# Attention operands split once and kept in DRAM, attention results in a buffer of their own, in a decoder-trunk kernel on one core

## What is computed

```python
def cross_attention(h, mem_n, wq, wk, wv, wo):
    ...
    s = jnp.einsum("bthd,bmhd->bhtm", q, k).astype(jnp.float32) * (XATTN_HEAD_DIM ** -0.5)
    p = jax.nn.softmax(s, axis=-1).astype(h.dtype)
    o = jnp.einsum("bhtm,bmhd->bthd", p, v).reshape(b, t, XATTN_HEADS * XATTN_HEAD_DIM)
    return o @ wo

def reference(...):
    ...
    h = rms_norm(x, xattn_pre_norm[l])
    y = cross_attention(h, mem_n, xattn_wq[l], xattn_wk[l], xattn_wv[l], xattn_wo[l])
    x = x + rms_norm(y, xattn_post_norm[l])
```

## Time and profile before

| | |
|---|---|
| time, 3 runs | 2698.38 us median (2696.05 to 2699.09) |
| profiled execution, its time | 2691.14 us |
| its span, first to last instruction | 2689.3 us |
| PE busy | 2549.9 us (95%) |
| DVE busy | 1579.4 us (59%) |
| ACT busy | 966.0 us (36%) |
| POOL busy | 982.5 us (37%) |
| mean granted TensorE clock | 0.984 of full speed |
| the four attention tiles | 782.72 to 1197.19 us of the span |

### The profile page before, as it was taken

The page is one execution under the profiler, slowest core; times in us unless marked ns, Lnnn a source line. Parts: engine busy times, 40 slices in busy tenths (PEclk is TensorE's granted clock), DMA queues, the critical chain, the costliest instruction groups (busy, mean ns, idle before and its releaser), DMA issues.

```text
span 2689.3 us, 33390 instructions
## 1 busy us (share of the span) xinstructions
PE 2549.9 (95%) x11713; PEld 2114.1 (79%) x11713; DVE 1579.4 (59%) x2446; ACT 966.0 (36%) x1565; POOL 982.5 (37%) x394
## 2 busy tenths in 40 slices
PE   7869899999998998999999999999999999999997
PEld 6657788878877787777888878888878888778886
DVE  4898888777736547447626456346276264562462
ACT  5323322232235444453433433333434334233332
POOL 6451400000023443333444444534444444345342
PEclk9989999999999999999999999999999999999999
DMA  8785585665834524435333244332353332443331
GB/s 243 232 317 196 196 302 177 240 251 209 307 125 172 195 79 179 166 95 185 95 110 94 81 142 147 109 94 95 87 189 96 107 94 84 133 128 107 91 94 63
DMA packets 318417, 410.59 MB, mean 153 GB/s; under 512 B 12584, under 2 KB 235069, under 8 KB 305469
## 3 DMA queue, kind: packets, MB, share of 16 engines
q1 hardware_dynamic: 309709, 396.62, 44.3%
q10 hardware_dynamic: 8560, 12.06, 1.3%
HBM read 343.62 MB, written 65.01 MB: 152 GB/s over the span
## 4 chain that ended last, share of the span: by engine, by line
PE 77%; DVE 14%; issue 5%; ACT 2%; DMA 1%; POOL 1%; DVEq 0%; ACTq 0%; SPq 0%; POOLq 0%
PE colb L1411 15%; PE colb L1413 15%; PE colb L1412 15%; PE accb L1411 10%; PE accb L1413 10%; PE accb L1412 10%; DVE arena L1147 3%; PE colb L1448 2%; DVE xh L1087 1%; DVE arena L1310 1%; DVE xh L1014 1%; DVE small L1008 1%; DVE small L1301 1%; ACT junk L656 1%; POOL pair L604 1%
## 5 line engine op out<-in xcount | busy, mean ns | idle before, releaser
L604 POOL TENSOR_TENSOR pair<-raw,pair 128x1024 fp32r<-128x1024 f32 x387 | 981.6, 2551 | 1676.2 <-ACT pair L635 1676.0
L1411 PE MATMUL colb<-hT,pair 128*128 128x512 f32 x1952 | 765.8, 392 | 18.8 <-issue 15.5
L1413 PE MATMUL colb<-hT,pair 128*128 128x512 f32 x1952 | 762.2, 390 | 0.0
L1412 PE MATMUL colb<-hT,pair 128*128 128x512 f32 x1952 | 762.0, 390 | 0.0
L635 ACT ACTIVATE pair<-raw 128x1024 fp32r<-128x1024 f32 x387 | 406.0, 1054 | 541.9 <-PE accb L1413 314.5
L1354 DVE TENSOR_SCALAR arena<-arena,par 128x512 f32<-128x512 f32 x176 | 246.1, 1438 | 375.5 <-ACT arena L938 375.0
L1411 PE MATMUL accb<-pair,act 128*128 128x512 f32 x1120 | 440.2, 393 | 18.7 <-issue 6.2
L1411 PEld LDWEIGHTS colb<-hT,pair 128*128 128x128 f32 x1952 | 368.3, 189 | 102.8 <-issue 27.1
L1413 PE MATMUL accb<-pair,act 128*128 128x512 f32 x1120 | 437.3, 390 | 0.0
L1412 PE MATMUL accb<-pair,act 128*128 128x512 f32 x1120 | 436.9, 390 | 0.0
L1413 PEld LDWEIGHTS colb<-hT,pair 128*128 128x128 f32 x1952 | 367.9, 188 | 77.5
(11 more groups left out here) (150 smaller groups left out, 2395.2 us busy)
## 6 DMA issues: line engine op xcount, KB each, us to landing
raw<-in_ffn_w_up SPq DMA_DIRECT2D x176, 512.0 KB, 3.8
pair<-kept SPq DMA_DIRECT2D x75, 1024.0 KB, 4.9
raw<-in_ffn_w_down SPq DMA_DIRECT2D x176, 256.0 KB, 2.9
kept<-pair SPq DMA_DIRECT2D x25, 1024.0 KB, 5.1
raw<-att_a SPq DMA_DIRECT2D x64, 256.0 KB, 3.0
raw<-att_b SPq DMA_DIRECT2D x64, 256.0 KB, 5.9
raw<-in_w_in SPq DMA_DIRECT2D x17, 512.0 KB, 6.6
xh<-in_x SPq DMA_DIRECT2D x4, 2048.0 KB, 14.2
```

Source lines behind the costliest of these rows:

```text
L604: nc.gpsimd.tensor_tensor(pair[:, b, 1, :], raw[:, r, :], pair[:, b, 0, :].bitcast(F32), ALU.subtract).then_inc(lo_done, 1)
L1411: nc.tensor.matmul(dst, sh, mh, start=first, stop=False)
L1412: nc.tensor.matmul(dst, sh, ml, start=False, stop=False)
L1413: return nc.tensor.matmul(dst, sl, mh, start=False, stop=last)
```

## The change

The 16 attention slots become kept slots too. The first attention tile is a stage of its own (`ATT_FIRST`): it loads and splits the slots as before, and SP stores each finished pair to `kept` (1 MB). The other three (`ATTN`) have no `hi` and no `lo`: SP loads the finished pair, as soon as PE has used the slot that had the buffer. Results go to `y_att`, a new part of the arena, and `xh` is loaded by `next_attended` in the tile before. In all tiles the first probability transposes come after slot 6 in place of slot 5. In `ATTN` the next rows' squares and scaling come before the exponentials and the first low parts, and their transposes one slot earlier; in `ATT_FIRST` their squares come after the rounding of the second transposes.

```diff
+    ORDER = {..., **{p: [("s", i) for i in range(2 * KD)] for p in ATTS}}
+    TILES = [1, 1, NT - 2, 1, 1, NT - 1, NT]
+    KEPT = [...] + [("s", i) for i in range(2 * KD)]
+    kept_in = {what: {"c": PREP, "s": ATT_FIRST}.get(what[0], MIX_FIRST) for what in KEPT}
+    HEADS_AT = {ATT_FIRST: 2, ATTN: 1}
+        y_att = part([RB, D])
...
+            def next_attended(tile):
+                sp.wait_ge(x_new, step_tile.at(ATT_FIRST, 0, 1))
+                sp.wait_ge(xp_full, xp.at(ATTN, tile - 1, 0) if tile else xp.at(ATT_FIRST, 0, 0))
+                if tile < NT - 1:
+                    sp.wait_ge(x_stored, 16 * (tile + 3))
+                    src = rows(x_mixed, tile + 1)
+                else:
+                    sp.wait_ge(x_stored, 16 * (2 + NT))
+                    src = rows(x_attended, 0)
+                sp.dma_start(xh[:, :, :], src).then_inc(xh_in, 16)
...
-                    if p == MIX_FIRST and i + LOAD_AHEAD - RAWS + 1 < SLOTS[p]:
+                    kept_next = i + LOAD_AHEAD - RAWS + 1
+                    if p in (MIX_FIRST, ATT_FIRST) and kept_next < SLOTS[p] or p == MIX_LAST and kept_next >= SLOTS[p]:
                         keep(p, t, i + LOAD_AHEAD - RAWS + 1)
                     load(p, t, i + LOAD_AHEAD, last)
+                    if p in ATTS and i == 9 and tile_of(p, t) < NT - 1:
+                        next_attended(tile_of(p, t) + 1)
...
-            for p in (MIX, MIX_LAST, ATTN, FFN):
+            for p in (MIX, MIX_LAST, ATT_FIRST, FFN):
                 with pool.Fori(0, TILES[p]) as t:
                     for n in range(len(SPLIT[p])):
                         lo(p, t, n)
...
                 for i in range(2 * KD):
-                    hi(ATTN, t, i + AHEAD)
+                    hi(p, t, i + AHEAD)
+                    if i == 2 and p == ATTN:
+                        next_squares(p, t)
                     if i == 3:
                         exps(0)
-                    if i == 5:
+                    if i == 6:
                         for k in range(4):
...
-                    if i == 6:
-                        next_squares(ATTN, t)
...
+                    if i == 8 and p == ATT_FIRST:
+                        next_squares(p, t)
...
-                take_rows(ATTN, t, 9, 15, 1, PV1_USE, xh)
+                take_rows(p, t, 9, 15, 1, PV1_USE, y_att)
...
                 normalise(0)
+                if p == ATTN:
+                    next_rows(p, t)
                 for k in range(4):
...
-                    if i == 5:
-                        pe.wait_ge(prob_ready, probs.at(ATTN, t, RB))
+                    if i == 6:
+                        pe.wait_ge(prob_ready, probs.at(p, t, RB))
```

More of the change, by code:

```diff
@@ L35 @@
 RSQRT_SEED = float(0x5F3759DF)
-PREP, MIX_FIRST, MIX, MIX_LAST, ATTN, FFN = range(6)
+PREP, MIX_FIRST, MIX, MIX_LAST, ATT_FIRST, ATTN, FFN = range(7)
 MIXES = (MIX_FIRST, MIX, MIX_LAST)
+ATTS = (ATT_FIRST, ATTN)
 RAWS = 4
@@ L131, in build @@
     KEPT = [("c", i) for i in range(CSLOTS)] + [("r", i) for i in range(RSLOTS)] +\
-           [("out", half, j) for half in range(2) for j in range(KD // 2)]
-    kept_in = {what: PREP if what[0] == "c" else MIX_FIRST for what in KEPT}
+           [("out", half, j) for half in range(2) for j in range(KD // 2)] + [("s", i) for i in range(2 * KD)]
+    kept_in = {what: {"c": PREP, "s": ATT_FIRST}.get(what[0], MIX_FIRST) for what in KEPT}
     def ready_made(p, i):
@@ L156, in stores_of @@
     def stores_of(b, p, i):
-        return 16 * sum(keeps(q, j) and pair_of[q][j] == b for q in (PREP, MIX_FIRST) for j in range(SLOTS[q]) if (q, j) < (p, i))
+        return 16 * sum(keeps(q, j) and pair_of[q][j] == b for q in (PREP, MIX_FIRST, ATT_FIRST) for j in range(SLOTS[q]) if (q, j) < (p, i))
     pool0, conf0, gate0 = 0, NP_, NP_ + NC_
@@ L199, in slot_source @@
                 return cols(w_in[0], REST_CHUNKS[n])
+            if what == "s":
+                half, j = divmod(n % KD, KD // 2)
+                return rows(lambda k: (att_a, att_b)[n // KD], (0, 2 * j, half), (0, 2 * j + 1, half))
             if what == "pooled":
@@ L208, in slot_source @@
             return rows(lambda k: pooled_w_out if k < NP_ else w_out[0], (0, Y_ORDER[2 * j], n), (0, Y_ORDER[2 * j + 1], n))
-        if p == ATTN:
-            half, j = divmod(i % KD, KD // 2)
-            return rows(lambda k: (att_a, att_b)[i // KD], (0, 2 * j, half), (0, 2 * j + 1, half))
         q, j = divmod(i, SLOTS[FFN] // 2)
@@ L223, in earlier @@
         if p > PREP and i < size:
-            before = bufs[p - 1] + bufs[p][:i]
+            before = sum(bufs[:p], []) + bufs[p][:i]
             d = min(d, next((e for e in range(1, 2 * size + 1) if before[-e] == own[j]), d))
@@ L412, in build @@
         pool_step = sem("pool_step")
-        nmaxs = Plan([0, 0, 0, 0, 8, 0], TILES)
-        probs = Plan([0, 0, 0, 0, 8, 0], TILES)
-        sigs = Plan([0, NC_, NC_, NC_, 0, 0], TILES)
-        sums = Plan([1, 1, 1, 0, 0, 0], TILES)
-        pairs = Plan([0] * 5 + [KF], TILES)
-        heads = Plan([2] + [1] * 5, TILES)
-        squares = Plan([M // P + RB] + [RB + 8] * 5, TILES)
+        nmaxs = Plan([0, 0, 0, 0, 8, 8, 0], TILES)
+        probs = Plan([0, 0, 0, 0, 8, 8, 0], TILES)
+        sigs = Plan([0, NC_, NC_, NC_, 0, 0, 0], TILES)
+        sums = Plan([1, 1, 1, 0, 0, 0, 0], TILES)
+        pairs = Plan([0] * 6 + [KF], TILES)
+        heads = Plan([2] + [1] * 6, TILES)
+        squares = Plan([M // P + RB] + [RB + 8] * 6, TILES)
         def result_squares(p, t):
@@ L541, in store_rows @@
                 sp.dma_start(rows(target[p], tile), xt[:, :, :]).then_inc(x_stored, 16)
+            def next_attended(tile):
[8 more added lines that the diff above has]
+                sp.dma_start(xh[:, :, :], src).then_inc(xh_in, 16)
             def body(p, t):
-                last = isinstance(t, int)
+                last = isinstance(t, int) and t == TILES[p] - 1
                 for i in range(SLOTS[p]):
@@ L557, in body @@
                         sp.dma_start(gain[:, :], post_gain[p][0].partition_broadcast(P)).then_inc(gain_in, 16)
-                        if not (last and p == FFN):
+                        if p not in ATTS and not (last and p == FFN):
                             sp.wait_ge(xp_full, xp.at(p, t, 0))
@@ L585, in _ @@
             body(MIX_LAST, 0)
-            for p in (ATTN, FFN):
-                with sp.Fori(0, NT - 1) as t:
-                    body(p, t)
-                body(p, NT - 1)
+            body(ATT_FIRST, 0)
+            for t in range(NT - 1):
+                body(ATTN, t)
+            with sp.Fori(0, NT - 1) as t:
+                body(FFN, t)
+            body(FFN, NT - 1)
             sp.wait_ge(x_stored, 16 * (1 + 3 * NT - 1 + RB))
@@ L1320, in attn @@
                 for k in range(4, KD):
[L1321 to L1322 removed]
+                    lo_acc(p, t, k, k % RB, act[:, 1, k, :], act[:, 0, k, :])
+                if p == ATT_FIRST:
+                    next_rows(p, t)
                 for k in range(KD):
[L1324 to L1325 removed]
+                    lo_acc(p, t, KD + k, k % RB, hT[:, 1, k, :], hT[:, 0, k, :], par_at[next_pre(p, t)] + k)
+                new_rows(p, t, y_att)
                 end()
[L1328 to L1330 removed]
+            attn(ATT_FIRST, 0)
+            with ve.Fori(0, NT - 2) as t:
+                attn(ATTN, t)
+            attn(ATTN, NT - 2)
             nc.vector.memset(halo[:, :, :], 0.0).then_inc(conv_ready, 1)
```

139 lines of the change are left out of this document (69 added, 70 removed).

## The result

| | before | changed |
|---|---|---|
| time, 4 runs each | 2697.22 us median (2694.32 to 2699.09) | 2663.03 us median (2660.64 to 2665.46) |
| profiled execution, its time | 2691.14 us | 2663.32 us |
| span | 2689.3 us | 2661.0 us |
| ratio changed/before | | 0.9874, 95% interval 0.9861 to 0.9888 |

The changed kernel is 34 us (1.3%) faster, by the interval 30 to 37 us. Repeated beside 23 and 9 fresh runs of the kernel before, the ratio was 0.9886 and 0.9889, which is 31 and 30 us. (One later execution of the changed kernel, of 5100.91 us, stands apart from all others, and the ratios leave it out.)

The account below looks back on a forecast made before the run. PE, 95% busy, was taken to bound the kernel, delayed by DVE, which POOL's splits slow. Tiles 1 to 3 give 26.0 us, tile 0 1.6: 2698.4 - 27.6 = 2670.8 us, range 2664 to 2684.

Parts of the forecast that it names:

- The lower end of the range: Whole kernel, 2664 us: all tiles at 94.6 would be 36 us less, tile 0's chain cuts that to 34.
- the 0.2 us: Tiles 1 to 3, PE's wait for `normalise(1)` before the second transposes: 0.2 us a tile counted, 0.5 kept as bound.
- The new wait for `xh`: Tile 0, PE before the next rows' transposes, their squares now coming later: 4.1 us, 6.5 or 2 as bounds.
- The second wait: Tile 0, PE before the second probability transposes: 2.2 us before, 1.2 us taken to stay, bounds 0 and 2.5.
- the first wait: PE before the first probability transposes, for `normalise(0)`: 4.4, 4.4, 2.5 us in tiles 1 to 3, 4.6 in tile 0, all gone.
- The DMA terms: Loads of finished pairs taken as 0 (bounds 0 and 1.3 us at three places a tile); tile 0's stores 0, bound 8.
- the 12.7 of the working: Load of a finished pair behind a 2 MB transfer: at most 12.7 us, needed three slots later, 16.3 us.
- One sign of being wrong: Listed signs: PE waiting for `pair<-kept`, ACT's squares for `xh` beyond 25 us, ACT for `raw` in tile 0, new FFN-head wait.
- `xh` late: Rival, chance 0.07: in tiles 1 to 3 `xh` lands at 31 us, not 13; 18 us in all, 2689.
- loads of pairs set the pace: Rival, chance 0.05: all loads on one queue; at 215 GB/s tiles take 110 us, tile 0 149; 2761 us.
- tile 0 pays: Rival, chance 0.13: a late load or store in tile 0 holds ACT's split and the exponentials; 10 to 12 us more, 2682.
- the change doesn't do what it says: Rival, chance 0.03: something other than POOL slows DVE, only the moved transposes give about 15 us; 2683.

Follow-up runs that it names:

- the move alone: Kernel before with one edit: first probability transposes after score slot 6 instead of 5, next rows' squares behind their rounding; 2688.18 us, ratio 0.9992.
- splits in every tile: Changed kernel without kept attention slots: every attention tile loads and splits them; order, result buffer and early load stay. 2675.05 us, ratio 0.9947 to the kernel before.
- late squares: Kernel splitting in all attention tiles, with tile 0's order in all four: next rows' squares behind the second rounding. 2686.74 us, ratio 0.9973 to the kernel before.
- the version with early squares: Changed kernel, in tile 0 next rows' squares behind the rounding of the first probability transposes; 2654.35 and 2656.27 us, ratios 0.9850 and 0.9867 to the kernel before.
- the kernel with POOL at work: Changed kernel plus one POOL subtraction per slot in tiles 1 to 3, in a buffer nothing else touches there; 2660.13 us, ratio 0.9874 to the kernel before.

## Why the prediction was right, and where it failed

**The step that failed** is the last of the sum: "The median of the runs is 7.2 us above the profiled time, and I subtract from it". The forecast is 7.8 us above the measured median. 2.7 of them are the sum (27.6 us forecast for the tiles, 30.3 measured); the other 5.1 are the time from which it was subtracted. 1.2 of these come from the three runs that I had, since with a fourth the median of the kernel before is 2697.2 in place of 2698.4. The last 3.9 are the difference between the kernels in this series, 34.2 us, over that of their tiles; in the later series it was 31 and 30. So the 7.2 us were no property of the kernel or of its profile. In later series the kernel before had medians of 2690.6, 2693.5 and 2693.5 (7 of its 61 executions there were as long as the shortest of the three, 2696.05), and its other profiled execution was 1 us above its own.

From the profiled execution the same working gives 2691.1 - 27.6 = 2663.5, 0.5 us from the median measured, and that is partly luck: its sum is 2.7 us too small, and in the changed kernel's profile the stages ahead of the tiles took 2.2 us more than in the profile before.

The attention tiles of equal kernels agree to 0.3 us in every pair of profiles, and the stretch behind them to 0.6 us in all 14 profiles (1491.7 to 1492.2). What varies lies ahead: the tiles begin at 778.5, 779.5 and 784.9 us in the changed kernel's three executions, at 782.7 and 785.3 in the two of the one before, and at 791.1 with the move alone, whose profiled execution was 8 us above its median. Why three runs of the first series were near 2698 stays open: no trace of them exists.

**The lower end of the range** does not come out of its own working: 26.6 us in tiles 1 to 3 and 6 in tile 0 are 32.6, not the 34 that were subtracted. The measured time lies below both.

**Tiles 1 to 3** were forecast at 94.6 us and 0.2, and took 94.1. A block of 16 transposes costs 1.77 us, (94.1 - 16 x 5.44) / 4, where I had worked out 1.9 from a place with a wait in it; the four blocks and the 0.2 us are the 0.7. Over three tiles this is 2.1 us, the sum's largest error of its own: the 28.1 us measured are the 26.0 forecast and this. Two readings on the way were wrong without harm. The end of the tile before starts on DVE 3.7 to 3.9 us into tiles 1 to 3, not 6.1, in the changed kernel, with splits in every tile and with late squares alike, and so in the changed kernel ends at 15.9 us, not 18.3; why it starts earlier stays open. And the scaling of the next rows contained two blocked operations, not one: it takes 5.1 us (912.88 to 918.00), not 7.3.

**Tile 0** was forecast at 102.5, and took 101.9, 101.6 and 101.8. The new wait for `xh` was 4.1 us by the working, 4.8 and twice 4.0 in the profiles, with a stretch of half clock of 3.4 us behind it in all three. The second wait was 0.4 to 0.9 in place of 1.2. The bound that its chain forbids more than 6 us held only for the late squares. I had costed the late squares of tile 0 rightly and not seen that they were needless: the version with early squares puts them back and gains 8.3 us over the kernel before in this tile.

**Why DVE is fast again** was right: POOL's work, not the order or the loads, decides the 20.5 or 12 us (12.0 without splits, 20.8 with them in the same order, 16.9 with work of POOL that touches nothing).

**Who gets the credit** was half wrong. I gave 26 us to the missing splits and the move "alone" 15. The move alone gave 2 (3 in the tiles), since the squares, which wait for `xh`, then delayed the second exponentials. Move, buffer and early squares together give 20 of the 30 us in the tiles, with all splits kept; the missing splits then add 10, or 12 with early squares in tile 0. By the time it is 14 of 31, with 5 us to either side. Taken the other way round, without splits the move is worth nothing in tiles 1 to 3. Each of the two removes the first wait by itself, and neither price is that of the whole.

**The DMA terms** at zero held: PE never waited for a finished pair, and the longest load of one in these tiles took 10.5 us, under the 12.7 of the working. One sign of being wrong did come: ACT waited for `raw` in tile 0 (10.5 us for `att_b`, three times, 4.4 for `att_a`; with splits and no stores 0.8). No cost of it shows: none of PE's waits is for it, and tile 0 without stores is no shorter. The rivals "`xh` late" and "loads of pairs set the pace" fell: ACT's squares began 13.8 us into tile 1 (900.55), and tiles 1 to 3 move 247 to 258 GB/s at a share of 0.7. So did "tile 0 pays", by the tile's 101.6 to 101.9 us, and "the change doesn't do what it says", by the kernel with POOL at work.

## What to carry to other kernels

Subtract a difference that comes from a profile from that profile's own time, and look at what varies between executions: here the stage in question repeats to 0.3 us, the FFN behind it to 0.6, and the stages ahead of it move by 6 in one and the same kernel. When two edits both cover one wait, try each alone before giving either the price: the wait moves to the next thing that is late, and only the second edit, which moves that thing too (here the squares ahead of the exponentials), brings it in. An engine with time to spare can still be worth relieving, if its operations hold up another's.

## What the runs showed of the hardware

- A POOL operation delays DVE operations even where they share no data, and however small they are: 0.17 us became 1.66 beside POOL operations of 1.9 us, and 128x4 operations of 0.16 us took 2.3 to 2.4 beside splits of 2.4 (with splits in every tile). The Trainium skill, "SBUF — State Buffer", section "Who interferes with whom", has this as an exclusive lock on a shared pair of ports that is held for a whole instruction; the trace agrees. It is not every operation. Those that were held up read SBUF alone. Those that read what PE wrote were not, and neither were the reciprocals (0.16 us) in SBUF: with POOL at work, 12 maxima of scores that ran beside it took 0.68 to 0.69 us like the 12 others, and 12 of the 24 low parts of `hT` 0.74 to 0.75 like the rest. And the one that starts second waits: POOL's operation of 893.64, which met a DVE operation already running, took 2.30 us in place of 1.90.

```profile
L1334 DVE TENSOR_REDUCE small<-accb x16: 678/692/693, 824.3 to 1119.4; 128x2 f32<-128x512 f32 x16
```

- Between waits of nearly equal length the clock differed: with splits in every tile PE waited 2.76 us in tile 1 and kept a granted clock of 1.00, waited 2.55 us in tile 2 and had 0.50, the 1.2 GHz level, for 3.4 us behind it, and that tile was 1.4 us longer.

```profile
937.94 1.31 PE L1642 MATMUL accb<-ident,arena 128*128 128x128 f32 x10 [2.76 <-DVE arena L1337]
...
1034.90 3.20 PE L1642 MATMUL accb<-ident,arena 128*128 128x128 f32 x16 [2.55 <-DVE arena L1337]
```

  The version that splits in every tile and squares early in tile 0 repeats it (97.21 and 98.58 us), and there a wait of 2.91 us in tile 0 left the clock at 1.00 too. So within 0.4 us the length of a wait did not decide; what did is not shown.
- The queues sustained 400 GB/s over 116 us. In the prediction I had set the 397 GB/s of the earlier trace rows against the figure of about 358 that the Trainium skill, "DMA: Bandwidth & Descriptors", gives for a core. The same page of the Trainium skill, in its section on measured bandwidth, has the 358 as what a core gets when both cores of a pair stream, and gives 425 GB/s for a load of 16 MB by a core alone. The 400 measured here, by one core with loads and stores mixed, lie near the second figure.
